# Third pair of output-projection strips by halves, moved splits, and a two-way end, in a one-core encoder layer

## The reference

```python
def swiglu_ffn(x, g, w_gate, w_up, w_down):
    h = rmsnorm(x, g)
    return (jax.nn.silu(h @ w_gate) * (h @ w_up)) @ w_down
...
xp = xp + 0.5 * swiglu_ffn(xp, *ffn1)
op, sp = mixer_prompt(rmsnorm(xp, norm_gains[l, 1]), *lw)   # h @ w_in, 32 heads of attention, o @ w_out
xp = xp + op
xp = xp + 0.5 * swiglu_ffn(xp, *ffn2)
```

## Time and profile before

| | |
|---|---|
| median of 3 runs | 2123.44 us (2122.14 to 2126.87) |
| the profiled execution | 2123.82 us |
| its span, first to last instruction | 2122.3 us |
| PE busy | 2105.8 us (99%) |
| DVE busy | 1168.8 us (55%) |
| ACT busy | 863.5 us (41%) |
| mean granted TensorE clock | 0.998 |
| HBM traffic | 160 GB/s over the span |

### The profile page before, as it was taken

How to read it: one execution, slowest core, us unless ns; L and a number is a source line. 1 busy time by engine, 2 the same in 40 slices (tenths; PEclk the granted TensorE clock), 3 DMA queues, 4 the chain that set the end, 5 groups by cost and what they waited for, 6 DMA issues and landing times.

```text
span 2122.3 us, 42683 instructions
## 1 busy us (share of the span) xinstructions
PE 2105.8 (99%) x15983; PEld 2077.7 (98%) x15983; DVE 1168.8 (55%) x1803; ACT 863.5 (41%) x1347; POOL 85.5 (4%) x128
## 2 busy tenths in 40 slices
PE   8999999999999999999999899999999999999999
PEld 8999999999999999999998899999999999999999
DVE  5555445554445556588878665555445554455543
ACT  5333333333333344445558544333333333333333
POOL 1000000000000000022332000000000000000000
PEclk9999999999999999999999999999999999999999
DMA  7556665655655656656574356665665565666564
GB/s 210 161 158 166 167 166 160 169 162 157 175 163 158 164 157 174 170 149 143 146 147 105 112 166 168 169 163 155 168 172 158 162 167 159 167 169 165 156 173 132
DMA packets 681999, 339.94 MB, mean 160 GB/s; under 512 B 59203, under 2 KB 679085, under 8 KB 681880
## 3 DMA queue, kind: packets, MB, share of 16 engines
q1 hardware_dynamic: 673816, 329.38, 57.7%
q0 software_dynamic: 2944, 7.47, 1.4%
q10 hardware_dynamic: 5184, 2.39, 0.4%
HBM read 334.46 MB, written 5.30 MB: 160 GB/s over the span
## 4 chain that ended last, share of the span: by engine, by line
PE 96%; SPq 1%; DVE 1%; ACT 1%; DMA 1%; issue 0%; ACTq 0%; DVEq 0%
PE bank L586 31%; PE bank L588 31%; PE bank L587 30%; PE bank L672 1%; PE bank L687 1%; PE bank L705 0%; PE bank L649 0%; DMA raw<-in_w_ffn_gate 0%; SPq L468 0%; DVE w_lo L1415 0%; ACT w_hi L1092 0%; PE bank L891 0%; SPq L503 0%; PE bank L656 0%; ACT gu_lo L1287 0%
## 5 line engine op out<-in xcount | busy, mean ns | idle before, releaser
L586 PE MATMUL bank<-h_hi,w_hi 128*128 128x288 f32 x3344 | 994.5, 297 | 1.3 <-DVE w_lo L1415 1.2
L587 PE MATMUL bank<-h_lo,w_hi 128*128 128x288 f32 x3344 | 986.9, 295 | 0.0
L588 PE MATMUL bank<-h_hi,w_lo 128*128 128x288 f32 x3344 | 983.7, 294 | 0.0
L1415 DVE TENSOR_TENSOR w_lo<-raw,w_hi 128x1024 fp32r<-128x1024 f32 (+2 forms) x642 | 738.4, 1190 | 259.7 <-ACT w_hi L1092 259.0
L1092 ACT ACTIVATE w_hi<-raw 128x1024 fp32r<-128x1024 f32 (+2 forms) x640 | 623.7, 1022 | 306.0 <-PE bank L588 267.4
L586 PEld LDWEIGHTS bank<-h_hi,w_hi 128*128 128x128 f32 x3344 | 627.1, 188 | 4.3 <-DVE w_lo L1415 1.7
L588 PEld LDWEIGHTS bank<-h_hi,w_lo 128*128 128x128 f32 x3344 | 630.2, 188 | 0.0
L587 PEld LDWEIGHTS bank<-h_lo,w_hi 128*128 128x128 f32 x3344 | 628.3, 188 | 0.1
L586 PE MATMUL bank<-gu_hi,w_hi 128*128 128x288 f32 x1376 | 408.1, 297 | 0.0
L587 PE MATMUL bank<-gu_lo,w_hi 128*128 128x288 f32 x1376 | 406.6, 296 | 0.0
L588 PE MATMUL bank<-gu_hi,w_lo 128*128 128x288 f32 x1376 | 406.5, 295 | 0.0
(11 more groups left out here) (241 smaller groups left out, 1001.4 us busy)
## 6 DMA issues: line engine op xcount, KB each, us to landing
raw<-in_w_ffn_gate SPq DMA_DIRECT2D x172, 512.0 KB, 4.9
raw<-in_w_ffn_up SPq DMA_DIRECT2D x172, 512.0 KB, 5.0
raw<-in_w_ffn_down SPq DMA_DIRECT2D x96, 512.0 KB, 4.1
raw<-in_w_in SPq DMA_DIRECT2D x74, 512.0 KB, 4.9
raw<-in_w_ffn_down SPq DMA_DIRECT2D x64, 384.0 KB, 4.7
raw<-in_w_ffn_down SPq DMA_DIRECT2D x32, 448.0 KB, 4.9
raw<-in_w_out SPq DMA_DIRECT2D x64, 96.0 KB, 2.6
raw<-in_w_out SPq DMA_DIRECT2D x32, 160.0 KB, 3.1
```

What stands on the lines that cost most here:

```text
L586: pe.matmul(out, w_hi[b][:, k, :], hi, start=(k == first_k), stop=False)
L587: pe.matmul(out, w_hi[b][:, k, :], lo, start=False, stop=False)
L588: mm = pe.matmul(out, w_lo[b][:, k, :], hi, start=False, stop=(k == last_k))
L1415: dve.tensor_tensor(w_lo[b][:, k, :], raw[b][:, k, :], w_hi[b][:, k, :].bitcast(F32), ALU.subtract)\
```

## The change

It has four parts.

- SP loads the third pair of wo strips, wo(2,0) and wo(2,1), by halves: tiles 8 to 15 of each (3 DMAs) when that half of the raw buffer is free, tiles 0 to 7 (6 DMAs) when the other is. New semaphores `ld_half` count the first halves. `part_used` is counted further, so that ACT may split half 0 of wo(2,0) while PE is still at the second halves of pair 1. Pair 2 is now written out on PE, ACT and DVE (`peel_first=3`). PE no longer waits for pair 1's products to be read before it begins pair 2, only for pair 0's, whose bank it takes.
- In `last_bodies` the split of a(1,0) moves to slots 0 and 1 on DVE and slot 0 on ACT; in slots 5 and 8 DVE does the second half of the next strip before `whole` and `inverse` instead of between the two inverses; in slot 11 the split of wo(1,1) stands behind both inverses.
- On DVE and ACT the splits of wo(2,0) stand earlier in phase wo, half by half.
- In the last phase the 15th strip is turned in the middle of the 16th strip's matmuls, and the 16th strip's rows go two ways: DVE adds the first 128 tokens alone, PE turns them into one bank, ACT copies and stores them; the second 128 tokens are turned into another bank and copied by DVE and stored by SP, and the 32 new tokens' rows are copied by DVE and stored by ACT.

```diff
                     wo = w_out[0]
 
+                    def wo_tiles(s, col, heads, first, last, landed, ph=ph):
+                        n = last - first
+                        if heads is None:
+                            r = (H_A + H_B) * HD + (first - 11) * P
+                            sp.dma_start(raw[buf(ph, s)][:, first:last, :],
+                                         wo[r:r + n * P, col].rearrange("(k p) n -> p k n", p=P)).then_inc(landed, 16)
+                            return
+                        for c in range(2):
+                            r = heads[c] * HD
+                            sp.dma_start(raw[buf(ph, s)][c * HD:(c + 1) * HD, first:last, :],
+                                         wo[r:r + n * HD, col].rearrange("(k p) n -> p k n", p=HD)).then_inc(landed, 16)
+
+                    def a_heads(s, col):
+                        for g in range(2):
+                            wo_tiles(s, col, (6 * g, 6 * g + 3), 3 * g, 3 * g + 3, ld_wo[s])
+
...
+                            a_heads(s, col)
+                            wo_tiles(s, col, (H_A, H_A + 5), 6, 11, ld_wo[s])
+                            wo_tiles(s, col, None, 11, 16, ld_wo[s])
                     wo_loads(0)
                     wo_loads(1)
-                    sp.wait_ge(lo_rdy, split_no(ph, 1, 0, 1))
-                    with sp.Fori(2, ph.strips // 2) as j:
+                    for half in range(2):
+                        for s in range(2):
+                            sp.wait_ge(lo_rdy, split_no(ph, 1, s, half))
+                            col = slice((4 + s) * P, (5 + s) * P)
+                            if half == 0:
+                                wo_tiles(s, col, (H_A + 2, H_A + 7), 8, 11, ld_half[s])
+                                wo_tiles(s, col, None, 11, 16, ld_half[s])
+                            else:
+                                a_heads(s, col)
+                                wo_tiles(s, col, (H_A, H_A + 5), 6, 8, ld_wo[s])
+                    with sp.Fori(3, ph.strips // 2) as j:
                         wo_loads(j)
+            sp.wait_ge(ys_cp, 1)
+            sp.dma_start(yp[0, P:2 * P, (DT - 1) * P:DT * P], y_rows[:, 1, 1, :]).then_inc(y_out[1], 16)
         WO_LOADS = 7
+
+        def wo_landed(j):
+
+            late = not isinstance(j, int) or j >= 2
+            return j * (16 * WO_LOADS) + 16 * (WO_LOADS - late)
...
+                        if isinstance(j, int) and j == 2:
+                            pe.wait_ge(evac, strip_no(ph, 0, s) + 1)
+                        elif bank is None:
...
-                        wo(1, 0, 5, 8)
+                        wo(1, 0, 5, 8).then_inc(part_used, 1)
...
-                wo(1, 1, 3, 8)
+                wo(1, 1, 3, 8).then_inc(part_used, 1)
                 wo(1, 0, 8, 16)
                 wo(1, 1, 8, 16)
-                with pe.Fori(2, phase["wo"].strips // 2) as j:
+                wo(2, 0, 0, 16)
+                wo(2, 1, 0, 16)
+                with pe.Fori(3, phase["wo"].strips // 2) as j:
                     wo(j, 0, 0, 16)
                     wo(j, 1, 0, 16)
...
+                    def down_end(ph, j, when):
+                        strip(ph, j, 0, gu_rhs, when)
+                        turn_y(ph, j * 2 - 1, 1)
+                        strip(ph, j, 1, gu_rhs, when, part=(0, 8))
+                        turn_y(ph, j * 2, 0)
+                        strip(ph, j, 1, gu_rhs, when, part=(8, None))
+                        pe.wait_ge(y_half, 1)
+                        pe.wait_ge(y_cp, DT - 2)
+                        pe.transpose(bank_t[1][:, 0:P], y_t[1][:, 0:P], ident[:, :]).then_inc(y_tr, 1)
+                        pe.wait_ge(evac, ph.n0 + DT)
+                        pe.transpose(bank_o[:, P:2 * P], y_t[1][:, P:2 * P], ident[:, :])
+                        pe.transpose(bank_o[0:T_S, 2 * P:3 * P], y_t[1][:, T_P:NT], ident[:, :]).then_inc(y_tr, 1)
...
                 if 0 in halves:
-                    if ph.name == "wo":
-                        act.wait_ge(ld_wo[s], j * (16 * WO_LOADS) + 16 * WO_LOADS)
+                    if ph.name == "wo" and isinstance(j, int) and j == 2:
+                        act.wait_ge(ld_half[s], 16 * 3)
+                    elif ph.name == "wo":
+                        act.wait_ge(ld_wo[s], wo_landed(j))
                     else:
                         act.wait_ge(ld[buf(ph, s)], loaded(ph, j, s))
-                    if ph.name == "wo" and isinstance(j, int) and j == 1:
-
-                        act.wait_ge(part_used, s + 1)
+                    if ph.name == "wo" and isinstance(j, int) and j in (1, 2):
+
+                        act.wait_ge(part_used, 2 * j + (s - 1))
                     elif not (isinstance(n, int) and n < 2):
 
                         act.wait_ge(used, n - 1)
-                elif ph.name == "wo" and isinstance(j, int) and j == 1:
+                if 1 in halves and ph.name == "wo" and isinstance(j, int) and j in (1, 2):
+                    if j == 2:
+                        act.wait_ge(ld_wo[s], wo_landed(j))
                     act.wait_ge(used, n - 1)
...
-                    if k == 1 and j < 3:
+                    if (v == 0 or k == 1 and 0 < j < 3):
                         split(run_strip(2 * j + 2), (0,))
                         split(run_strip(2 * j + 2), (1,))
+                    if k == 1 and j < 3:
                         split(run_strip(2 * j + 3), (0,))
                     elif k == 1 and j == 3:
                         split((phase["wo"], 1, 0), (0,))
...
-                                if j == 1 and s == 1:
-                                    split(following(ph, j, s))
+                                    split((ph, 2, 0), (0,))
+                                if j == 1 and s == 0:
+                                    split((ph, 2, 0), (1,))
                             else:
                                 split(following(ph, j, s))
                             if h_after:
...
+                        cols = slice((DT - 1) * P, DT * P)
+                        act.wait_ge(y_tr, DT)
+                        act.wait_ge(y_out[1], (DT - 2) * 16)
+                        act.activation(y_rows[:, 1, 0, :], bank_t[1][:, 0:P], ACT.Copy).then_inc(y_cp, 1)
+                        act.wait_ge(y_cp, DT)
+                        act.dma_start(yp[0, 0:P, cols], y_rows[:, 1, 0, :]).then_inc(y_out[1], 16)
+                        act.wait_ge(ys_cp, 2)
+                        act.dma_start(ys[0][:, cols], y_rows[0:T_S, 1, 2, :]).then_inc(y_out[1], 16)
...
@@ -1579,22 +1634,24 @@
                     smax(*unit(g1))
                     if k < 2 and j:
                         out_lo(j + 3, k, run_tile(j + 3, k))
+                    if k == 2 and 0 < j < 3:
+                        part(2 * j + 2, 1)
                     if k and j < 3:
                         whole(j, k - 1)
                     inverse(*unit(g0))
                     if k == 0 and j:
                         part(2 * j + 1, 1)
-                    if k == 2 and j < 3:
-                        part(2 * j + 2, 1)
-                    if k == 2 and j == 3:
-                        split((phase["wo"], 1, 1), (0,))
                     inverse(*unit(g1))
-                    if k == 1 and j < 3:
+                    if v == 0:
+                        part(2, 0)
+                    elif v == 1:
+                        part(2, 1)
+                    elif k == 1 and j < 3:
                         part(2 * j + 2, 0)
-                    if k == 1 and j == 3:
-                        split((phase["wo"], 1, 0), (0,))
-                    if k == 2 and j < 3:
+                    elif k == 2 and j < 3:
                         part(2 * j + 3, 0)
+                    elif k:
+                        split((phase["wo"], 1, k - 1), (0,))
...
-                            if not early or (j, s) == (1, 1):
+                            if not early:
                                 split(following(ph, j, s))
                             dve.wait_ge(used, n + 1)
...
+                            if final and isinstance(d, int) and d == DT - 1:
+                                dve.scalar_tensor_tensor(dst[:, 0:P], bank_w[buf(ph, s)][:, 0:P], factor, xT[:, d, 0:P], ALU.mult, ALU.add)\
+                                   .then_inc(y_half, 1)
+                                dve.scalar_tensor_tensor(dst[:, P:NT], bank_w[buf(ph, s)][:, P:NT], factor, xT[:, d, P:NT], ALU.mult, ALU.add)\
+                                   .then_inc(evac, 1)
+                                dve.wait_ge(y_tr, DT + 1)
+                                dve.wait_ge(y_out[1], (DT - 2) * 16)
+                                dve.tensor_copy(y_rows[:, 1, 1, :], bank_o[:, P:2 * P]).then_inc(ys_cp, 1)
+                                dve.tensor_copy(y_rows[0:T_S, 1, 2, :], bank_o[0:T_S, 2 * P:3 * P]).then_inc(ys_cp, 1)
+                                continue
```

(10 more changed lines are left out.)

25 lines of the change are left out of this document (7 added, 18 removed).

## The result

| | before | after |
|---|---|---|
| median of the first five runs | 2123.44 us | 2112.34 us (2111.31 to 2114.53) |
| ratio, with its 95% interval | | 0.995 (0.9939 to 0.996) |
| all unedited runs of the study | 2122.39 us (69 runs) | 2112.34 us (15 runs) |
| the profiled execution, its span | 2123.82, 2122.3 us | 2114.53, 2113.0 us |
| mean granted clock | 0.998 | 1.000 |

The change makes the kernel 11.1 us faster by the first runs, 10.05 us (95% interval 8.5 to 11.1, from resampling the runs) by all. In the three comparisons of the unedited pair it was 11.1, 8.8 and 10.7 us faster (the first runs, e5 and e16).

A forecast was written before the change was run, and what follows sets the result against it. PE was taken as the bound, busy 99% of the span, so only its gaps, slow matmuls and end could be won. 1.5 + 0.2 + 0.2 + 5.7 + 1.0 = 8.6 us off gave 2115.0 us, range 2113.2 to 2119.3.

The forecast's parts named there:

- The baseline step: Tied the forecast to a median of 2123.44 us, with the profiled execution of 2123.82 us 0.38 above it.
- Slots (A): Second norm to last attention output: moved splits save 1.5 us in slot 3, 0.2 in slots 5 and 8, 0.2 in slot 12.
- Slot 3: PE's wait for the second half of a(1,0) goes through the earlier split: 1.5 us saved, bounds 1.0 to 1.5.
- The second half of a(2,0): Slots 5 and 8: this half is split before `whole` and `inverse`; 0.18 us lost there, 0.2 forecast, bounds 0 to 0.3.
- Slot 12: PE's 1.11 us gap for a normalised probability shrinks by 0.2 us, limited by ACT's exponentials; bounds 0 to 1.11.
- a short wait costs no clock: PE's waits of 1.23 and 1.11 us were said to be followed by matmul steps of 0.13 us again.
- The long gap (B): Before wo(2,0): 4.37 us of waiting and 1.63 of slow clock go, 0.3 comes back; net 5.7, bounds 2.3 to 6.0.
- The step that failed is the landing of wo(3,0)'s last load: The last of wo(3,0)'s 7 DMAs lands 3.5 us after its issue; strip ready at 1217.3, wanted at 1217.24.
- mild late supply: Half 1 of wo(2,0) lands 2 us late: 2116.7 us, or 2118.3 if the clock falls too; chance of late supply 0.26.
- the first rival: Half 1 of wo(2,0) lands 1.5 to 2.5 us late because wo(2,1)'s loads share the DMA engines; chance 0.26.
- The other two rivals: Nearly the old wait returns at wo(2,1), 2120.5 us, chance 0.09; strips from wo(3,0) on wait for loads, 2127.9, chance 0.03.
- The end (C): Last phase: turning strip 15 earlier and strip 16's rows two ways saves 1.0 us, bounds 0 to 1.5.

The follow-up runs named there:

- e5: The changed kernel again, nothing edited; 2113.32 us, 8.8 below the before of its group.
- e16: The changed kernel again, unedited, on the chip of e13 to e15; 2111.80 us.
- e2: The kernel before with only the moved splits of slots 0 to 2, 5, 8 and 11; 2119.84 us, 2.6 faster.
- e4: The changed kernel with the old end; 2113.61 us, 8.9 below before.
- e6: The changed kernel with two of the six loads of wo(2,0)'s second half issued on ACT's queue instead of SP's; 2111.94 us.
- e8: The changed kernel with ten matmuls into an unused bank ahead of the first norm; 2113.03 us.
- e10: The changed kernel with wo(2,1) loaded whole by 7 DMAs, wo(2,0) still by halves; 2112.80 us.
- e14: The kernel of e9 again, on the chip of e13; 2112.36 us.
- e9: The changed kernel with ACT squaring all of x before it waits for the third strip's load in the start; 2111.71 us.
- e1: The kernel before with only the new end; 2121.64 us, 0.8 faster.
- e3: The kernel before with only the third pair loaded and split by halves; 2116.99 us, 5.5 faster.
- e11: The kernel before with 24 matmuls filling PE's long wait ahead of wo(2,0); 2120.90 us, 0.45 below before in its group.
- e13: The kernel before with e9's edit, the start's squares moved ahead of the split; 2121.38 us.
- e12: The changed kernel with the edits of e6, e7 and e9 together; 2110.77 us.
- e15: The kernel of e12 again; 2111.23 us.
- e7: The changed kernel with ACT's split of wo(1,1)'s first half moved one slot later; 2111.60 us.

## Why the prediction was off by 2.7 us

The miss of 2115.0 - 2112.34 = 2.66 us is in two parts that add exactly: the median of before that it was tied to stood 2123.44 - 2122.39 = 1.05 too high, and the change is worth 10.05 instead of 2123.44 - 2115.0 = 8.44, 1.6 more. Of that, 0.16 is rounding: 8.6 off 2123.44 is 2114.84.

Of the signs that the prediction named, most came: no wait for `w_lo` from 1100 to 1210, steps of 0.13, no fall of the clock, 1.56 us at the end. Two did not. The gap in slot 12 is 0.72 for 0.8 to 1.0, and from wo(2,0)'s first matmul to wo(3,0)'s it is 1214.80 - 1201.06 = 13.74 us, over the 13.5.

**The baseline step failed.** "That execution stands 0.38 above the median of the runs" took three runs for the kernel's time. The profiled execution had a long start: N1 is 856.46, and the median of the twelve unedited starts is 854.4. Between 852.7 and 857.2 the start alone moves by 4.5 us, through a clock that falls behind PE's wait for the norm in some executions and through transposes that take longer in others. The range held the bounds of the terms and nothing for this. Tied to 2122.39, its lower end would be 2112.15, and the measured time would lie above it.

**Slots (A): forecast 1.9, measured 2.4 to 3.0.** Slot 3 gave its 1.5: steps of 0.13, and after the mark the pieces before it match to 0.01 us. The second half of a(2,0) gave its 0.18. Slot 12 was mis-sized: I took 0.2 because the exponentials end late on ACT. But ACT was late since it stood in a split for wo(1,1)'s DMA, and by how much differs between executions; with DVE's split out of the way the gap was 0 to 1.0 in ten profiles, 0.4 on the mean, not 0.9. The mean A of nine profiles with the new order (after, e2, e4, e5, e6, e8, e10, e14, e16; e9 with its fall elsewhere left out) is 334.06; of the old order without a fall (before, e1, e3) 336.50, which is 2.4, and of all five of the old order 337.07, which is 3.0.

The difference of these two, 0.6 us, is a sentence of mine that fell: "a short wait costs no clock". It rested on one execution, and on a row of the slot-3 wait alone. Two of the five profiles of the old slot 12 (e11 and e13) have the clock at 0.50 behind it, and none of the profiles of the new one. The mean clock of the timed runs fits, though it doesn't say where a fall was, and one in the start lowers it too: of 64 runs of before that list it, 22 have 0.997, with a median of 2124.3, and 13 have 0.999, with 2120.8. The changed kernel has 1.000 in 10 of 15, median 2111.8.

**The long gap (B): forecast 5.7, measured 5.0 to 5.5** (mean 95.42 of the ten with halves, against before's 100.47 or the mean of before, e1, e2 and e13, 100.91). Its 6.0 went: in e12 and e15, where nothing comes back, B is 6.0 below before's. The clock's 1.6 in it was 1.45 by e11. But 0.9 came back at wo(3,0) and not 0.3. The step that failed is the landing of wo(3,0)'s last load: 5.1 us after its issue for the 3.5 assumed, partly made good because it was issued 0.65 earlier than I had it (counted from wo(2,0)'s start). The size is that of a mild late supply, but not by the first rival's way: it had half 1 of wo(2,0) late, and that came early. The other two rivals did not occur either: no wait in wo(2,1), and no wait for a strip from wo(3,1) on.

**The end (C): forecast 1.0, measured 0.9**; 1.56 us from read to issue, forecast 1.6.

Together the measured terms are 2.4 + 5.5 + 0.9 = 8.8 without, 9.4 with the slot-12 falls, in place of 8.6. The rest to 10.05, 0.6 us, stays open: 9.4 is inside the interval of the difference (8.5 to 11.1), and the falls in the start, in four of twelve profiles with the unedited start (before, e1, e5, e7), are in both kernels.

**Fewer and larger DMAs.** The rule that the forecast quotes from the Trainium skill, "DMA: Bandwidth & Descriptors", section Rules for kernel authors, would have had the 18 DMAs of the third pair lose against 14 or 16. In sum e10 shows neither gain nor loss from two fewer. What e6 shows to count is how many stand in SP's list between a buffer's release and its strip's last load, at 12.72 / 18 = 0.7 us each; it took two of them elsewhere and the wait went. The late landing of wo(3,0)'s last load stayed in e6 (5.2 us) and was shorter in e10 (3.8).

## What to carry to other kernels

Where a kernel's time differs by 2 us between executions, cut the profiles at marks in code that is not edited, and compare stretch by stretch: that separates a change of 2.4 us from a start that moves by 4.5. Tie a forecast to many runs, and put the spread of executions into the range beside the bounds of the terms. A wait of about 1 us that one profile shows without a fall of the clock can have one in the next; count it with a chance.

## What was not expected of the hardware

- PE's wait of 1.0 to 1.4 us in slot 12 is followed by some 3 us at a granted clock of 0.50 in two of five profiles. The wait of 1.23 us in slot 3 has no fall in the same five. The step into wo(3,0) was 0.6 to 1.2 us too long in nine profiles, and none had it. Ahead of the first norm, waits of 1.1 to 1.6 us had it in one of five profiles (e1; not e3, e4, e11, e16), and the three of 2.8 to 2.9 us (before, e5, e7) all had it.
- In the start, 54 transposes take 6.2 to 6.6 us in eleven profiles (before 6.21) and 8.0 to 9.9 in seven (after 9.86), with a granted clock of 1.00 written beside both. The same window of PE's timeline, first before, then after:

```profile
10.00:11.00 1.00, 1.00 (x10) 1.00 1.13 349
```

```profile
10.00:11.00 1.00, 1.00 (x6) 1.00 1.13 345
```

PE is busy in both, with 10 matmuls and with 6. The traces have no record of the clock there: the first one begins at 4.5 us before and at 14.2 us after, at 4.5 to 7.3 us in all of the eleven and at 10.4 to 14.2 us in all of the seven, and ahead of it the column says 1.00. So in these first 15 us the column tells nothing, and the long transposes go with a late first record.

- e9's fall at 1062 us has no wait of PE beside it in the list of waits: PE is busy in the windows before it. Its cause was not looked for.
